# Block 2 of a two-block sequence model: the keys of head pairs 2 and 3 move out of attention into a fifth Strassen pair, and every attention step takes 13 filling products

## The reference

```python
h = rms_norm(x, ln1_g)
z = h @ w_in + b_in                      # 1024 -> 5632 features
q, k, v, u, y_branch, g_att, g_rec = split(z)     # q, k, v: 512 each, 8 heads of 64
y_att = neighbourhood_attention(q, k, v, rpb) @ w_att_o
...                                      # recurrent branch y_rec
mixed = sigmoid(g_att) * y_att + sigmoid(g_rec) * y_rec
x = x + mixed @ w_out
```

## Time and profile before

| | |
|---|---|
| runs | 2752.88, 2752.89, 2753.04 us; median 2752.89 |
| the profiled execution | 2752.42 us, of which the span from the first to the last instruction is 2750.6 |
| TensorE matmul | busy 2742.4 us of the span, at a granted clock of 1.00 |
| VectorE, ScalarE, GpSimd | 1925.1, 1389.6 and 108.5 us busy |
| block 2, the four Strassen pairs | 1352.9 to 1428.9 us of the span |
| block 2, attention steps 0 to 31 | 1437.0 to about 1633.8 us |

### The profile page before, as it was taken

The page is one execution under the profiler, slowest core; times in us unless marked ns, Lnnn a source line. Parts: engine busy times, 40 slices in busy tenths (PEclk is TensorE's granted clock), DMA queues, the critical chain, the costliest instruction groups (busy, mean ns, idle before and its releaser), DMA issues.

```text
span 2750.6 us, 35028 instructions
## 1 busy us (share of the span) xinstructions
PE 2742.4 (100%) x13140; PEld 2241.7 (81%) x13140; DVE 1925.1 (70%) x2769; ACT 1389.6 (51%) x2240; POOL 108.5 (4%) x105
## 2 busy tenths in 40 slices
PE   9999999999999999999999999999999999999999
PEld 8888877788888888888887778888888888888887
DVE  8877656765866667688956653889546866667796
ACT  7332566423645554453446551888424655544454
POOL 0000112000000000000003320000000000000000
PEclk9999999999999999999999999999999999999999
DMA  4333433433433385551352121122223343384441
GB/s 162 117 112 110 166 108 108 149 104 138 148 145 153 140 307 191 158 159 33 138 178 62 55 76 48 55 57 60 82 77 142 138 150 153 138 331 163 157 153 66
DMA packets 102342, 356.58 MB, mean 130 GB/s; under 512 B 10784, under 2 KB 10912, under 8 KB 96032
## 3 DMA queue, kind: packets, MB, share of 16 engines
q1 hardware_dynamic: 100880, 349.63, 36.5%
q10 hardware_dynamic: 1296, 4.72, 0.5%
HBM read 251.54 MB, written 102.76 MB: 129 GB/s over the span
## 4 chain that ended last, share of the span: by engine, by line
PE 98%; DVE 1%; ACT 0%; issue 0%; DMA 0%; SPq 0%; POOL 0%; DVEq 0%; ACTq 0%; POOLq 0%
PE ps L523 17%; PE ps L3482 12%; PE pa L3874 11%; PE ps L3874 11%; PE ps L3903 9%; PE pa L3903 9%; PE pa L3519 6%; PE ps L3519 5%; PE pa L523 4%; PE ps L3789 2%; PE pa L3610 2%; PE ps L3991 2%; PE ps L3923 2%; PE pa L3655 2%; PE pa L3621 1%; PE pa L3633 1%
## 5 line engine op out<-in xcount | busy, mean ns | idle before, releaser
L1785 ACT ACTIVATE krh<-k_rraw 128x512 fp32r<-128x512 f32 x192 | 121.1, 631 | 254.3 <-PE ps L3903 120.5
L513 DVE TENSOR_TENSOR w_lo<-w_raw,w_hi 128x1024 fp32r<-128x1024 f32 (+1 forms) x100 | 119.6, 1196 | 140.6 <-ACT w_hi L507 140.4
L2879 DVE TENSOR_TENSOR krl<-k_rraw,krh 128x512 fp32r<-128x512 f32 x192 | 132.6, 691 | 117.7 <-ACT krh L1785 117.5
L507 ACT ACTIVATE w_hi<-w_raw 128x1024 fp32r<-128x1024 f32 (+1 forms) x100 | 101.7, 1018 | 196.6 <-PE ps L523 112.2
L523 PE MATMUL ps<-a_hi,w_hi 128*128 128x512 f32 x576 | 177.5, 389 | 0.0
L523 PE MATMUL ps<-a_hi,w_lo 128*128 128x512 f32 x576 | 177.3, 389 | 0.0
L523 PE MATMUL ps<-a_lo,w_hi 128*128 128x512 f32 x576 | 177.3, 389 | 0.0
L3874 PE MATMUL pa<-xh,fwh 128*128 128x512 f32 x448 | 174.5, 390 | 0.0
L3874 PE MATMUL ps<-xh,fwh 128*128 128x512 f32 x448 | 174.3, 389 | 0.0
L3874 PE MATMUL pa<-xh,fwl 128*128 128x512 f32 x448 | 174.3, 389 | 0.0
L3874 PE MATMUL ps<-xh,fwl 128*128 128x512 f32 x448 | 174.3, 389 | 0.0
(11 more groups left out here) (500 smaller groups left out, 6786.6 us busy)
## 6 DMA issues: line engine op xcount, KB each, us to landing
w_raw<-wstream SPq DMA_DIRECT2D x100, 512.0 KB, 3.6
k_rraw<-hff SPq DMA_DIRECT2D x192, 256.0 KB, 2.7
hff<-hbuf SPq DMA_DIRECT2D x32, 1024.0 KB, 3.9
wA<-wff SPq DMA_DIRECT2D x16, 2048.0 KB, 7.7
hff<-hbuf SPq DMA_DIRECT2D x32, 768.0 KB, 3.2
w_raw<-wff SPq DMA_DIRECT2D x32, 512.0 KB, 4.3
f_raw<-wff SPq DMA_DIRECT2D x32, 512.0 KB, 4.5
proj<-res SPq DMA_DIRECT2D x24, 512.0 KB, 5.9
```

The lines of the kernel that those rows point to most:

```text
L507: nc.scalar.activation(w_hi[:, slot, 0:n], w_raw[:, slot, 0:n], ACT.Copy).then_inc(s_whi, 1)
L513: nc.vector.tensor_tensor(w_lo[:, slot, 0:n], w_raw[:, slot, 0:n], w_hi[:, slot, 0:n].bitcast(F32), ALU.subtract).then_inc(s_wlo, 1)
L1785: nc.scalar.activation(k_r[e % 4][0][:], k_rraw[:, e % 4], ACT.Copy).then_inc(sem("s_khi"), 1)
L2879: nc.vector.tensor_tensor(k_r[e % 4][1][:], k_rraw[:, e % 4], k_r[e % 4][0][:].bitcast(F32), ALU.subtract).then_inc(sem("s_klo"), 1)
```

## The change

The keys of head pairs 2 and 3 leave the attention stage. They become a fifth Strassen pair, placed last, whose bias is added by `pair_gate` with Identity in place of Tanh, and are kept in `gates` in DRAM. SyncE loads each into its place in `qk2` once the scores of the pair that used the place are done. Attention now has 14 units instead of 16, in the order v0 q0 k0 v1 q1 k1 v2 q2 v3 q3 and four extras, and every one of steps 0 to 31 takes 13 filling products. Since the number of pairs is now odd, PSUM banks, output places and semaphores swap parity, also in the MLP that follows; the first pair now uses the banks of `ps`. With five pairs `w_raw` is in use up to pair 4, so the loads of the weight tiles of units 4 and 5 move into the last pair, ahead of the bias tiles.

```diff
-P2_UNITS = [("a", n) for n in (4, 5, 6, 7)] + [("r", n) for n in (4, 5, 6, 7)]
+P2_UNITS = [("a", n) for n in (4, 5, 6, 7)] + [("r", n) for n in (4, 5, 6, 7)] + [("k", 2), ("k", 3)]
+UNITS2 = [("v", 0), ("q", 0), ("k", 0), ("v", 1), ("q", 1), ("k", 1), ("v", 2), ("q", 2), ("v", 3), ("q", 3)]
...
                 if i + 2 < N_PROJ2:
                     proj_load(i + 2, 2)
-                elif i + 2 == N_PROJ2:
+                if i == LASTP2:
                     for m in range(2):
                         load_unit(sp, u + AHEAD + m, m)
-                if i == LASTP2:
                     for o in range(2):
                         bias_load(o)
...
-            units(u + 6, u + 18)
+            units(u + 6, u + 10)
+            sp.wait_ge(sem("s_hst0"), 32 * ((PB2 + N_PROJ2 + 1) // 2))
+            sp.wait_ge(sem("s_S"), (N_PAIR1 + 1) * UNITS_PER_PAIR)
+            sp.dma_start(qk2[:, 0, 1], gates[P2_UNITS.index(("k", 2))]).then_inc(sem("s_ldq0"), 16)
+            units(u + 10, u + 12)
+            sp.wait_ge(sem("s_S"), (N_PAIR1 + 2) * UNITS_PER_PAIR)
+            sp.dma_start(qk2[:, 1, 1], gates[P2_UNITS.index(("k", 3))]).then_inc(sem("s_ldq1"), 16)
+            units(u + 12, u + 16)
...
             if b == 2:
-                return 17 if s < 24 else 13 if s < 32 else 20
+                return 13 if s < 32 else 20
...
         def scored_unit(s):
 
-            m = unit_at(2, s) if s >= 0 else None
-            which, p = unit_of(m) if m is not None else (None, None)
-            return (p, which - 1) if which in (1, 2) else None
+            for at, n in ((s, 0), (s - 1, 1)):
+                m = unit_at(2, at) if at >= 0 else None
+                which, p = unit_of(m) if m is not None else (None, None)
+                if which == 2 and n == 0:
+                    return p, 1
+                if which == 1 and (n == 0 or p >= 2):
+                    return p, n
+            return None
```

More of the change, by code:

```diff
@@ L82 @@
 U_OUT = 8
[L83 removed]
+U_ATT2, U_GAT0, U_REC, U_MRG2 = len(UNITS2) + EXTRA, 4, 25, 11
 SPREADS = (1, 2, 3)
@@ L965, in unit_of @@
         def unit_of(m):
-            return divmod(m, 3)[::-1] if m < 3 * N_PAIR2 else ("extra", m - 3 * N_PAIR2)
+            if m >= len(UNITS2):
+                return "extra", m - len(UNITS2)
+            kind, p = UNITS2[m]
+            return "vqk".index(kind), p
         def score_operand(b, p, n):
@@ L1160, in proj_copy @@
                 dst, src = {0: (p_p1[:], 0), 1: (p_p5[:], 2), 4: (p_p7[b], 3)}[n]
-                nc.scalar.activation(dst, proj_bank(i, src), ACT.Copy).then_inc(sem("s_pcp"), 1)
+                nc.scalar.activation(dst, proj_bank(i, src, b), ACT.Copy).then_inc(sem("s_pcp"), 1)
             def pair_gate(i, o, c, made, at=2):
-                n = {"a": 4, "r": 12}[P2_UNITS[2 * i + o][0]] + P2_UNITS[2 * i + o][1]
-                dst = proj_out(i)[:, o, half(c)]
+                kind, n = P2_UNITS[2 * i + o]
+                if kind == "k":
+                    how, kw = ACT.Identity, {"bias": V("b_in", 4 + n)}
+                else:
+                    n += {"a": 4, "r": 12}[kind]
+                    how, kw = ACT.Tanh, {"scale": 0.5, "bias": hb[:, n:n + 1]}
+                dst = proj_out(i, 2)[:, o, half(c)]
                 if (o, c) == (0, 0):
@@ L1172, in pair_gate @@
                         act.wait_ge(sem("s_stored"), 64)
-                    nc.scalar.activation(dst, proj_bank(i, 0), ACT.Tanh, scale=0.5, bias=hb[:, n:n + 1]
-                                         ).then_inc(sem("s_pj11"), 1)
+                    nc.scalar.activation(dst, proj_bank(i, 0, 2), how, **kw).then_inc(sem("s_pj11"), 1)
                     return
                 act.wait_ge(sem("s_fc"), 3 * (PB2 + i) + made)
-                nc.scalar.activation(dst, dst, ACT.Tanh, scale=0.5, bias=hb[:, n:n + 1]).then_inc(sem("s_pjsc"), 1)
+                nc.scalar.activation(dst, dst, how, **kw).then_inc(sem("s_pjsc"), 1)
             def first_operand_hi(p, n):
@@ L1398, in operand_hi @@
                         act.wait_ge(sem("s_ldq0"), 144 + 32)
+                    elif p >= 2 and n:
+                        act.wait_ge(*((sem("s_ldq0"), 144 + 48) if p == 2 else (sem("s_ldq1"), 144 + 32)))
                     else:
@@ L1523, in second_attention @@
                 a2_hi(npair - 1)
-                unit_hi(3 * npair + EXTRA - 1)
-                unit_out(3 * npair + EXTRA - 1)
+                unit_hi(U_ATT2 - 1)
+                unit_out(U_ATT2 - 1)
             def pool_hi(t):
@@ L4095, in weight_stream @@
     w = i["w_in_2"][0]
-    for p in range(N_PAIR2):
-        for c in (8, 0, 4):
-            out[:, u] = tiles(w, c + p)
-            u += 1
+    for kind, p in UNITS2:
+        out[:, u] = tiles(w, {"v": 8, "q": 0, "k": 4}[kind] + p)
+        u += 1
     for n in range(EXTRA):
@@ L4142, in projection_weights @@
     for j, (kind, n) in enumerate(P2_UNITS):
-        out[:, N_PROJ + j // 2, j % 2] = tiles(w2, {"a": 28, "r": 36}[kind] + n)
+        out[:, N_PROJ + j // 2, j % 2] = tiles(w2, {"k": 4, "a": 28, "r": 36}[kind] + n)
     return out.reshape(P, N_PROJ + N_PROJ2, 2, S)
```

65 lines of the change are left out of this document (35 added, 30 removed).

## The result

The changed kernel takes 2759.26 us (median of 14 runs, 2756.27 to 2760.67), the kernel before 2752.78 (14 runs, 2751.9 to 2753.04): ratio 1.0023, 95% interval 1.0016 to 1.0031. It is slower by 6.5 us, just over the 0.2% that can be told from no change. The profiled execution took 2758.8 us. The new thing beside the median is the spread: 4.4 us between the runs of the changed kernel, 1.1 between those of before.

A forecast was written before the change was run, and what follows sets the result against it. TensorE was taken to set the time. Fifth pair +19.0, attention -17.0 and k's DMA delay +2.9 made +4.9 us: 2757.3 for the profiled execution, 2757.8 for the median, range 2753.5 to 2761.8.

The forecast's parts named there:

- k's load: Before unit 4: 1.05 MB more queued ahead of k makes it land later, costing 2.9 us; bounds 0 and 3.6.
- The fifth pair: End of the Strassen pairs: one more pair of 84 matmuls adds 19.04 us.
- What a step gives back: Attention steps 0 to 23: four fewer fillers shorten steps by 0.73 to 0.94 us each, 21.7 together.
- The new hold-ups: Attention: ScalarE's lists run over into shorter steps, chiefly delaying steps 11, 14, 18 and 22; loss 4.7 us.
- The clock: Rival, after the gap before unit 4: TensorE's clock falls to half, adding 3.7 us, 2761.5; chance 0.17.
- Counting holds: Rival: ScalarE's hold-ups don't come and k is not later, so matmul count alone gives -2.7 us, 2750.2; chance 0.06.
- No DMA delay: Rival: attention as forecast but k lands as before; +2.0 us, 2754.9; chance 0.17.
- Edits at nothing: Bank parity in pair 0, Identity for Tanh, MLP semaphore parity: no cost; 1.1 us if pair 0 waited.
- On order in the queue: DMA queue before unit 4: engines consume descriptors in ring order, so the whole 1.05 MB stands ahead of k.

The follow-up runs named there:

- four-pair kernel: Kernel before with only the weight loads of units 4 and 5 moved into the last Strassen pair, ahead of the bias tiles: 2753.92 us, ratio 1.0006.
- The filled gap: Changed kernel with 12 additional unused matmuls between the last Strassen product and unit 4, DMA as it was: 2757.35 us, ratio 1.0018.
- four such edits: Changed kernel with bias and mask tiles behind v, plus o_out, a2 pieces and unit_hi later, and 14 and 12 fillers per even and odd step: 2750.89 us.
- its sister with a gap of 1.8: Kernel before with weight loads moved, last pair's results stored in the changed kernel's places and the pairs' weight array one pair longer: 2754.72 us, ratio 1.0008.
- the keys first: Changed kernel with the Strassen pairs reordered: the pair with the keys runs first and a gate pair last: 2758.74 us, ratio 1.0023.

## Why the prediction was right, and where its sum was off

2757.8 was predicted with a range of 2753.5 to 2761.8; measured 2759.26. The mechanisms named did come, but two of the sums came out partly by luck: in attention two errors cancelled, and in k's load a cause came in that was not foreseen.

- **The fifth pair, +19.0.** 19.04 us, and 136.41 us from step 0 to step 24 where 136.4 was written. Counting filling products against the pair would have promised 2.7 us less than before.
- **What a step gives back.** Even steps 4.80, odd 6.07, odd with a batch 6.50 (6.46), even with a batch 5.04 (4.99). The 0.20 that four fewer fillers don't give back in an even step is what the version with 14 and 12 fillers takes back: the fourteenth costs 0.03. Without the hold-ups the steps gave back 21.1, for 21.7.
- **The new hold-ups, 4.7.** Steps 11, 14, 18 and 22 were named, and no others are held up. They cost 1.12, 1.12, 0.77 and 1.12, 4.1 together, for 1.3, 1.1, 1.0 and 1.1; step 3 lost nothing. That attention as a whole gave back 16.9 for 17.0 is luck in part: the 0.6 too much in what the steps give back and the 0.6 too much in the hold-ups cancel. The copy of step 14 came at 2.59 after the scores, to the digit. Step 11's first exp came at 3.41, not 3.65. That it is the length of ScalarE's list was shown by taking items out of it: `o_out` moved 0.48 us from the steps after odd lists to step 11, and `unit_hi` took 0.47 to 0.81 from all four. Two of the items gave less than their own length (`a2_hi` 0.67 and `unit_hi` 0.47 to 0.81 of 0.95). For `unit_hi` the steps had hardly more to give: they were 0.92, 0.89, 0.48 and 0.89 over their kind. The edits of `a2_hi` and `unit_hi` moved a part of VectorE's work too; only the one of `o_out` is ScalarE's alone.
- **k's load, +2.9.** 10.23 us for k's DMA (about 10), and 2.7 more wait ahead of unit 4. Moving other bytes behind k took the wait away; adding 1 MB ahead added 2.4. But the size is right by luck in part: the same 1.05 MB cost only 1.4 us in the four-pair kernel. Which result the last pair computes and its places in DRAM are excluded. The streams part at the stores of the gates, where in the changed kernel an instruction packet keeps one DMA engine for 0.96 us; in the prediction's sum there was no such term. So "2.9 from the DMA rate" is more than the bytes themselves cost: 1.4 us in one case and 2.4 in another, and 2.7 with the packet between them.
- **The clock: the term that the sum lacked.** It was written as a rival at 0.17, worth +3.7, and left out of the sum. It is no either-or. The profiled run had it, at 1.60. The filled gap takes 1.6 us off the median, and with it the spread. By their times, 9 of the changed kernel's 14 runs (2758.8 to 2760.67) had the fall and 5 (2756.27 to 2757.81) did not; in those five, with a median of 2757.51, the sum's 2757.8 would have been right to within 1.5. Only the profiled run was seen to fall; for the others it is an inference from their times. The place named was right (the gap ahead of unit 4), and with the gap filled the ratio is 1.0018 where it was 1.0023. In the profiled run the price was less than 3.7 because the low level lasts some 3 us, not the whole 7.4 up to step 0. But that run is the fastest of the nine, whose median is 2760.3, 2.8 above that of the five. With 1 MB more ahead the low level lasted longer and cost 2.0. So 1.6 is the low end of the price; whether the dearer runs fell for longer or waited longer for k, no trace shows. On the rule of the Trainium skill (TensorE: Matmul & The Clock Gate, "What's actually happening"): the fall to half after idling and the return after work are both in the stretches above. The same section of the Trainium skill has the monitor run freely, unaligned to the kernel, which fits that one kernel falls in some runs and not in others.
- **The other rivals.** "Counting holds" fell with the four long steps. "No DMA delay", written as 2754.9, is what the version with the bias tiles behind v makes true on purpose: 2754.39.
- **Edits at nothing.** The first pair starts at 1352.80 (1352.86 before), and nothing waits in it. The wait of 1.0 ahead of the MLP is as before.
- **On order in the queue.** The rule cited from the Trainium skill (DMA: Bandwidth & Descriptors, "Queues, rings and completion order") puts all that is issued ahead of k in front of it. The trace agrees in direction: behind k, 1.4 MB cost nothing. The 1.4 and 2.7 us for the same bytes show that the size does not follow from the bytes ahead alone.

Together: the DMA delay and what hangs on it cost 4.6 of the 6.5 us, shown by one experiment; the other 1.9 (2754.39 against 2752.47) are a pair that costs more than the steps give back, 19.0 for 16.9. The attention part alone would need shorter ScalarE lists to pay: with four such edits 3.5 us more came back.

## What to carry to other kernels

Moving products from filling slots into a dense block gives up their cover: count first which engine's list had been hidden under them, step by step, by starts and not by busy shares. When a load is moved next to one that is already just in time, price the delay, and then ask what the gap that it opens does to TensorE's clock; order the queue by what is wanted first, and if a gap must stay, keep TensorE at work in it. A step that waits for another engine anyway takes one more filling product for nothing, and the neighbour may have one less.

## What the runs showed of the hardware that I had not expected

- The granted clock fell after a gap of 1.9 us (the profile of the four-pair kernel with its loads moved; by the times in 3 of its 11 runs, and in 5 of 10 of its sister with a gap of 1.8) and stayed at 1.00 after one of 3.4 us (the profile with the keys first). At 3.2 to 3.4 us it fell in 16 of 23 runs by their times, at 5.6 in the profile, and the other four runs lie within 0.8 us of it; with waits of 0.2 to 0.6 us no kernel has such a split. The length of the gap alone does not decide.
- A short gap costs twice: 3.2 us idle, and in the profiled run 1.6 more in products at 1.2 GHz behind it (2.0 behind the gap of 5.6 us).
- 1.05 MB queued ahead of a load delayed its user by 1.4 us in one program and 2.7 in another, with the same transfers in the same order around it and equal rates (316 and 325 GB/s). In the second a 16 KB instruction packet kept one of the 16 DMA engines for 0.96 us between them; every transfer that landed after it was 0.3 to 1.5 us later than in the first. That the packet is the cause is read from five traces and not tested.
